# Two expert layers of a 512-token block: numbers of eight heads in one call, every second first-quarter batch of one-hots on ACT, blocks weighed by pairs

## What is computed

```python
q = (xb @ w_q).reshape(PEER_BLOCK, PEER_HEADS, 2, PEER_HALF)           # 8 heads, 2 halves of 128
s = jnp.einsum('thpd,hpnd->thpn', q, sub_keys)                         # 128 keys for each half
s_top, i_top = lax.top_k(s, PEER_TOPK)                                 # 16 of 128
cand = s_top[:, :, 0, :, None] + s_top[:, :, 1, None, :]
cand_idx = i_top[:, :, 0, :, None] * PEER_N_KEYS + i_top[:, :, 1, None, :]
best, pos = lax.top_k(cand.reshape(...), PEER_TOPK)                    # 16 of 256
expert = jnp.take_along_axis(cand_idx, pos, axis=-1)
g = jax.nn.softmax(best, axis=-1)
act = gelu(jnp.einsum('td,thkd->thk', xb, u[expert]))
out = jnp.einsum('thk,thkd->td', g * act, v[expert])
```

## Time and profile before

| | before |
|---|---|
| median of 3 runs | 3348.59 us (3344.89 to 3349.8) |
| the profiled execution's own time | 3350.17 us |
| its span, first to last instruction | 3348.4 us |
| mean granted clock of TensorE | 0.961 of 2.4 GHz |
| busy: PE, DVE, ACT, POOL | 92%, 74%, 39%, 40% of the span |
| moved by DMA | 931 MB, 278 GB/s on the mean |

### The profile page before, as it was taken

One profiled execution on the slowest core, in us unless ns is written; L12 is line 12 of the kernel. 1 busy time (PEld: TensorE's weight loads), 2 busy tenths in 40 slices (PEclk: granted clock), 3 DMA queues, 4 the chain that ended last, 5 costly groups with the idle time before them and its releaser, 6 DMA issues. The chain is left out here.

```text
span 3348.4 us, 46062 instructions
## 1 busy us (share of the span) xinstructions
PE 3096.9 (92%) x16440; PEld 2061.0 (62%) x16440; DVE 2462.3 (74%) x5627; ACT 1311.1 (39%) x3317; POOL 1342.1 (40%) x1040
## 2 busy tenths in 40 slices
PE   7999899789999998989699999997899999999887
PEld 2466488656666666655344554786666666666553
DVE  5874369979799788877721253599888898788777
ACT  3232122476556555500101162224675565555100
POOL 0000000536566677767300000005356567667765
PEclk9999999899999999999899989998899999999999
DMA  8510262869999999999812101527789999999998
GB/s 293 186 51 26 95 226 70 302 221 391 387 372 400 409 398 409 409 409 409 340 56 82 59 11 38 201 70 269 249 341 392 368 399 408 396 409 409 409 409 346
DMA packets 282683, 931.23 MB, mean 278 GB/s; under 512 B 31804, under 2 KB 32460, under 8 KB 281944
## 3 DMA queue, kind: packets, MB, share of 16 engines
q0 software_dynamic: 147840, 536.96, 41.1%
q1 hardware_dynamic: 134616, 391.34, 31.1%
HBM read 921.87 MB, written 6.32 MB: 277 GB/s over the span
## 5 line engine op out<-in xcount | busy, mean ns | idle before, releaser
L739 PE MATMUL psum<-hT,mod 128*128 128x256 f32 x4096 | 983.0, 395 | 56.5 <-ACT big L1197 52.7
L739 PEld LDWEIGHTS psum<-hT,mod 128*128 128x128 f32 x4096 | 791.7, 198 | 182.4 <-issue 76.1
L1207 ACT ACTIVATE levels<-key_numbers,hT 128x128 bf16<-128x128 f32 x1712 | 541.7, 388 | 318.2 <-PE psum L775 318.2
L1860 DVE SCALAR_TENSOR_TENSOR tmp<-w,small,tmp 128x1024 f32<-128x1024 f32 x339 | 435.8, 1285 | 68.1 <-DMA w<-in_peer_up,tmp 32.9
L2035 POOL DMA_INDIRECT w<-in_peer_u,tmp x172 | 237.3, 1380 | 595.0 <-DVEq L1688 457.8
L1840 DVE CUSTOM_DVE_ANT_0 w<-w,hn 128x1024 f32<-128x1024 f32 x342 | 408.8, 1224 | 70.2 <-DMA w<-in_peer_u,tmp 36.6
L2035 POOL DMA_INDIRECT big<-in_peer_down,tmp x86 | 116.1, 1350 | 722.3 <-DVEq L1688 645.2
L749 PE MATMUL psum<-rows,big 128*128 128x512 f32 x768 | 345.4, 593 | 4.1 <-DVE big L1793 4.1
L775 PEld LDWEIGHTS psum<-x,levels 128*128 128x128 bf16 x6144 | 226.7, 101 | 187.6 <-issue 133.2
L775 PE MATMUL psum<-x,levels 128*128 128x32 bf16 x6144 | 238.3, 196 | 70.3 <-issue 30.8
L1223 ACT ACTIVATE small<-small 128x4 f32<-128x4 f32 x128 | 26.3, 205 | 641.3 <-DVE small L1840 641.2
(11 more groups left out here) (324 smaller groups left out, 4278.7 us busy)
## 6 DMA issues: line engine op xcount, KB each, us to landing
mod<-in_uT SPq DMA_DIRECT2D x256, 512.0 KB, 6.8
rows<-in_peer_v SPq DMA_DIRECT2D x64, 512.0 KB, 6.8
rows<-in_peer_up SPq DMA_DIRECT2D x64, 512.0 KB, 6.8
w<-in_w_in SPq DMA_DIRECT2D x14, 2048.0 KB, 8.3
srow<-in_peer_v SPq DMA_DIRECT2D x32, 512.0 KB
tmp<-in_peer_v SPq DMA_DIRECT2D x32, 512.0 KB
srow<-in_peer_up SPq DMA_DIRECT2D x32, 512.0 KB
tmp<-in_peer_up SPq DMA_DIRECT2D x32, 512.0 KB
```

The costliest lines, as they stand in the source:

```text
L739: last = nc.tensor.matmul(ps[4 + e % 2][:, 0:ND], ub[e % UV][:, k, :], hT[:, k, ND:SEQ], start=k == 0, stop=k == KC - 1)
L1207: last = nc.scalar.activation(hits[n % HITS][:, j * P:(j + 1) * P], keyno, ACT.Abs, bias=nibT[:, n * BATCH + j:n * BATCH + j + 1])
L1860: last = stt(y, row, c8[g % 2][:, b:b + 1], y, ALU.mult, ALU.add)
```

## The change

1. `numbers` is called for all eight heads of tiles 2, 3 and 0 at once, after all four pairs of heads. Its one-hots of 16 x 128 elements lie in a new tile `wide_onehot`, KB 8 to 11 of `x`'s room, so DVE waits for `x_stored` before the first such call instead of before `key_rows`. The gates of these tiles are started and finished in one part. Tile 1 keeps its two parts and the old tile.
2. `by_scalar` gives ACT every second batch of the first quarter instead of every third: 32 of 64, not 22.
3. `weigh_block` becomes `weigh_pair`: one instruction for two blocks, every second block; `WEIGHED` goes from 3 to 4.
4. The tables: up to four more batches are due from block 10 on (44 instead of 40 by block 16), so all 192 are done by block 90 instead of 92. Copies come earlier: the 16 of a quarter by block 26 instead of 29, the 32 by 58 instead of 61. A copy at an even block `e` waits for `blk_ready` up to `e + 6`, which is the pair weighed in that block; before it needed `e + 2` or less. The planner counts 0.45 instead of 0.61 for DVE's weighing.

```diff
-WEIGHED = 3
+WEIGHED = 4
...
 def by_scalar(q, n):
 
-    return q > 0 or n % 3 == 0
+    return q > 0 or n % 2 == 0
...
 def batches_due(e):
 
-    return 0 if e < 0 else min(LATER, 2 * e + 4 + min(4, e // 2))
+    return 0 if e < 0 else min(LATER, 2 * e + 4 + min(8, e // 2))
...
 def copies_due(e):
 
-    return 0 if e < 0 else min(LATER // 4, (e + 1) // 2 + 1)
+    return 0 if e < 0 else min(LATER // 4, e // 2 + 3, batches_due(e + 1) // 4)
...
-        other = 0.61 + 1.69 * (spreads_due(e) - spreads_due(e - 1)) + 1.25 * (pieces_due(e) - pieces_due(e - 1))
+        other = 0.45 + 1.69 * (spreads_due(e) - spreads_due(e - 1)) + 1.25 * (pieces_due(e) - pieces_due(e - 1))
...
+        wide_onehot = part(x_, 8, 4, BF16)
...
+        def zg_pair(e):
+
+            n = e if e < len(zg_first) else (e - len(zg_first)) % ZG
+            if e < len(zg_first):
+                v = part(x_, n, 2).rearrange("p (e n) -> p e n", e=2)
+            elif n < 4:
+                v = hT[:, 3 + n:5 + n, 0:ND]
+            else:
+                v = part(big, 16 + n - 4, 2).rearrange("p (e n) -> p e n", e=2)
+            return v.rearrange("p e (j i) -> p e j i", i=8)
...
-                oh = onehot[:, 0:slots * TOPK]
+                oh = (wide_onehot if count == NH else onehot)[:, 0:slots * TOPK]
...
-                for h0, h1 in ((0, EARLY_HEADS), (EARLY_HEADS, NH)):
+                for h0, h1 in ((0, EARLY_HEADS), (EARLY_HEADS, NH)) if t == 1 else ((0, NH),):
...
-                    if p == 2:
-                        for t in DENSE:
-                            at_once(numbers(t, 0, EARLY_HEADS))
+                dve.wait_ge(x_stored, 16 * NT * (layer + 1))
                 for t in DENSE:
                     start_gates(t)
-                    at_once(numbers(t, EARLY_HEADS, NH))
+                    at_once(numbers(t, 0, NH))
...
-                at_once(numbers(0, 0, EARLY_HEADS))
-                at_once(numbers(0, EARLY_HEADS, NH))
+                at_once(numbers(0, 0, NH))
                 expert_rows(0)
                 finish_gates(0)
-                dve.wait_ge(x_stored, 16 * NT * (layer + 1))
...
-                def weigh_block(e):
+                def weigh_pair(e):
+
                     at = layer * NKEY + e
                     q, j = divmod(e, QA)
                     if j == 0:
                         dve.wait_ge(ga_copied, (layer * QUARTERS + q + 1) * WIDES)
-                    dve.wait_ge(blk_gelu, at + 1)
-                    z = zg(e).rearrange("p (j i) -> p j i", i=8)
-                    tt(z, z, gates[q % 2][:, j, :, :], ALU.mult).then_inc(blk_ready, 1)
+                    dve.wait_ge(blk_gelu, at + 2)
+                    z = zg_pair(e)
+                    tt(z, z, gates[q % 2][:, j:j + 2, :, :], ALU.mult).then_inc(blk_ready, 2)
...
-                for e in range(WEIGHED):
-                    weigh_block(e)
+                for e in range(0, WEIGHED, 2):
+                    weigh_pair(e)
                 for e in range(NKEY):
-                    if e + WEIGHED < NKEY:
-                        weigh_block(e + WEIGHED)
+                    if e % 2 == 0 and e + WEIGHED < NKEY:
+                        weigh_pair(e + WEIGHED)
```

## The result

The changed kernel takes **3332.51 us** (median of 7 runs, 3329.8 to 3336.97) where the kernel before took 3350.21 (7 runs): ratio 0.9949, interval 0.9939 to 0.996. That is -17.7 us, faster by 0.5%, in the range, and about half of what was forecast (-33, 3316 us). The profiled execution took 3334.3 us with a span of 3332.5; before, 3350.2 and 3348.4.

What follows compares the result with a forecast made beforehand. No one engine was the bound: limits differ by stage, and time won ahead of block 64 moves the end. Terms -11 - 6 + 1 + 1.5 - 2 = -16.5 us a layer, -33 in both, gave 3316 us; range 3294 to 3338.

Steps and rivals of the forecast that it cites:

- Term 1: Choice and start of first quarter: eight-head numbers let gate products start near 588.7 instead of 600.0; -11 us a layer.
- the line through two call lengths: Choice: from six-head and two-head calls, 0.065 us a slot, so 12.25 us for 128 slots against 16.17.
- The wait for x set aside: Choice: moved ahead of the numbers, costed at nothing; if the store were late, each us lost in full.
- Term 2: First quarter: DVE's second keys go from 42 batches to 32; -6 us a layer, bounds 0 and -7.5.
- The first rival: First quarter: ACT sets the pace, every second batch comes late; -10.5 us a layer, 3328 in all; chance 0.20.
- Term 3: Ramp, blocks 0 to 7: one more copy of gates, 1.05 us of ACT; +1 us a layer.
- Term 4: By block 16 PE has done four more batches, in the stage PE bounds; +1.5 us a layer.
- Term 5: Middle: quarter-ending copies come sooner, shortening DVE's stops, whose cost is DMA time; -2 us a layer, bounds 0 and -12.
- the rival in which it fills the middle: Middle: DVE no longer stops, gathers run full, term 5 is -12; -26.5 us a layer, 3296; chance 0.15.
- Weighing by pairs: Blocks: spares DVE 0 to 39 us a layer, counted as nothing because PE and waits for rows hide it.
- The slower rival: Middle: copies at even blocks wait for DVE's weighing and hold PE; +13 us a layer, 3375; chance 0.06.
- gaps of PE between blocks 8 and 63: Middle: a sign listed as showing the prediction wrong; blocks were expected to stay 7.73 us apart.

Runs made afterwards that it cites:

- late copies: Changed kernel with `copies_due` bound by `batches_due(e)` instead of `batches_due(e + 1)`, so copies wait only for batches already made: 3317.58 us, ratio 0.99.
- early copies without pairs: Kernel before with numbers of eight heads and every second batch on ACT, plus the changed kernel's `copies_due` line: 3417.49 us, ratio 1.0184.

## Why the prediction was half right

*Term 1, start of the first quarter, -11.* Right in the choice. From a layer's first choice to its rows chosen took 142.5 us before and 131.9 after, in both layers. The numbers of a tile with what follows take 12.6 us (513.10 to 525.75), against 12.25 from the line through two call lengths; gate product 0 comes at 590.5 instead of 600.0 (forecast 588.7), and alone the part gave -21 in both layers. The wait for x set aside cost nothing.

*Term 2, every second batch on ACT, -6.* Right: -6.0 in layer 1, -8.2 in layer 2, -11 alone in both. DVE was the bound of that stage, with ACT's spare time hidden in waits for PE. The Trainium skill, ScalarE: Activation LUTs, section Rules for kernel authors, advises against relu on this engine. The trace agrees that a batch costs ACT three times as much (1.90 against 0.65 us) and disagrees that this decides: a batch went to an engine that had room. The first rival falls.

*Term 3, one more copy in the ramp, +1.* **The price of the earlier copies is the step that failed**, here and in term 4. I charged one copy its own 1.05 us of ACT, charged the others nothing, and never asked what a copy waits for. Its price is not its length but the wait for PE and what is queued behind it. The ramp took 3.6 and 1.8 us more than before. Against the kernel whose copies wait for batches already made (46.4 us) it is 2.4 us more at nearly the same clock (layer 2, 0.97 against 0.96); the larger part of layer 1's 5.3 is the lower clock, and that the copies brought it is not shown.

*Term 4, four more batches, +1.5.* The batches are as priced: blocks 8 to 16 take 63.4 us with them and late copies, 62.2 without, +1.2. But the stage got 6.0 and 6.2 us longer, since the four early copies of blocks 9 to 14 lie in it, 1.2 us each (68.3 against 63.4 us). Terms 3 and 4 together were forecast at 5 us for both layers and measured 17.6; these 12.6 us are most of the miss, and some 2 of them are the clock in layer 1's ramp (the same work keeps PE busy 45.5 us there, 43.3 before).

*Term 5, DVE's stops at the quarters, -2.* Right in size: DVE's wait for copies fell from 25.3 to 4.4 us, and blocks 16 to the end became 1.5 and 2.8 us shorter. DMA moved 396 GB/s in blocks 16 to 64 instead of 391, not the rest's 407, and the end came 1.5 and 2.8 us sooner and not 12, so the rival in which it fills the middle falls.

*What is left, 5 us.* Layer 2's start came 5.5 us sooner, not 11. From the end of layer 1's blocks to the rows of layer 2 the kernels with the numbers of eight heads took 628.8 to 636.1 us (this one 634.3), those without 639.7, 642.0 and 645.8. The saving is in all of them; the scatter of 7 us is in the mixer, where the mean granted clock of a 40 us stretch falls to between 0.53 and 0.70 in the first one, and is 1.00 in others, in every run. I didn't settle what places the low stretches.

*Weighing by pairs, nothing.* Right for the time. That DVE's shorter work is hidden was argued and is not shown by itself: with this table of copies, pairs also keep ACT's copies from waiting for the weighing, 5.5 us of PE in blocks 16 to 64 that the rest gives back. A pair takes 1.05 us against 0.606 for one, near the upper bound. The Trainium skill, VectorE: DVE Perf Modes, section The TRN2 errata, would make it 0.69; the measurement decides.

*The slower rival* had the right shape, a copy on ACT with work queued behind it, and a wrong releaser for this kernel: in the ramp and the middle no copy waits for DVE's weighing, and I did not look at its other operand, PE's batches. I had read `copies_due` against what DVE needs, not against `batches_due(e + 1)`. In the rest there is one such wait a layer, in layer 1:
```profile
1339.57 1.05 ACT L1229 ACTIVATE big<-psum 128x512 f32<-128x512 f32 x1 [4.71 <-DVE big L1802]
```
The margin before was one block and not two: a copy at an odd block `e` needed the block that DVE weighs at `e - 1`. With blocks weighed one by one the feared wait is there in number (71 us of ACT's in layer 1's blocks 16 to 64). It exists the other way round too, DVE waiting for the copy, and costs 10 to 13 us if pairs come without more batches. The sentence that gaps of PE between blocks 8 and 63 would prove me wrong was the useful one: they were there.

## What to carry to other kernels

When an order is written out as a table of due times, check each new due time against the producer's table at the same step: an item that is due one step before its producer is done stops its in-order engine, and all that is queued behind it, gelus and freed PSUM banks included. The price is the length of the stop as the *bottleneck* feels it (1.6 us), not the waiting engine's (8 us) and not the item's own (1.05 us). And take a change of several parts apart early: here two small parts of it give the whole gain (3316 us), the rest adds nothing measurable, and one bound in that rest takes 15 us back (3332).

## What was unexpected of the hardware

Widening an fp32 DVE operation from 256 to 512 elements, in this weighing's layout, took 1.05 us against 0.606: only 13% is saved by joining two. The hits kept their price however the load was split between the engines: 0.687 to 0.689 us a batch on DVE and 0.388 to 0.391 us for each of ACT's four instructions on one token, with 42 or 32 of a quarter's 64 batches on DVE. And 43 us of PE's time in one layer, in the kernel with early copies without pairs, hung on an engine that its page shows 39% busy. The same eight matmuls took 6.56 us in one layer and 3.68 in the other after the same waits, at the two levels of the granted clock.
